# Constant products on TensorE around the router of a two-layer decoder trunk: 25 for 14 ahead of the rank products, and nine new ones behind them

## The chip, the cores and the metric

The kernel runs on one core of one Trainium2 chip. The metric is the device time of one execution in microseconds (us), lower is better. TensorE (PE in the profile) multiplies, VectorE (DVE) and ScalarE (ACT) work on vectors, GpSimd (POOL) is nearly unused, and SyncE (SP) issues the loads of the weights.

## The reference, cut to what matters

All of it is float32, with 256 tokens, a width of 1024, two layers, and 32 experts in 4 groups of 8.

```python
for l in range(DEPTH):                       # DEPTH = 2
    x = x + token_mixers(rms_norm(x, norm_mix_g[l]), ...)
    h = rms_norm(x, norm_ffn_g[l])
    glog = h @ rg_w + rg_b                   # 4 group logits, the best group is taken
    elog = h @ re_w + re_b                   # 32 expert logits, the best 2 of that group are taken
    # every token goes to its two experts; the tokens of an expert are ordered (rank within the expert)
    # expert e, for its tokens:  (silu(xb @ w_gate[e]) * (xb @ w_up[e])) @ w_down[e]
    # the weighted results are added to x
return rms_norm(x, norm_final_g)
```

## The kernel before, in words

Every engine has a program of its own that runs in the order in which it is written; semaphores join them. A layer has two parts. The first, the mixers, multiplies by the combined projection and its successors (function `product`, line 1362). The second is the mixture of experts: all 32 experts are gone through in pairs of experts, 16 pairs a layer, each with 64 places for tokens, and one more passage of the same loop where an expert has more tokens. The weights of a pair are 12 blocks of 1 MB, loaded by SP (line 502) into a ring of 18 slots. SP loads into a slot again when TensorE has counted `pair_freed` for it (lines 461 and following).

The change lies between the two parts, in `tensor_program` (from line 1338). In the order in which TensorE has it, for each layer:

- `norm_transposes(1)` (line 1392) transposes `x`.
- 16 products of the router (line 1578) give the 36 logits of each token in psC, and count `route_ps`. VectorE waits for that and works out the groups and the experts of each token in a chain of small operations, lines 1162 to 1194. The last of them writes `member`, a table of tokens by experts, and counts `members`. In the trace `member` has the name `ycT_parts`, and the tables beside it have the name `ycT`.
- `spin(14)` (function at line 1374, body at line 1377) makes 14 products of the constants `ones` and `before` (128x128 each) into the first quarter of psD's second half, `psD[:, 1, 0:128]`. Nobody reads it; the next to write there is the pair's own turning of its selection (line 1654), on TensorE too.
- TensorE waits for `members`, and makes five rank products (line 1586) into the first half of psD, and counts `rank_ps`.
- VectorE, which has meanwhile worked out the weights of the experts (lines 1197 to 1203), waits for `rank_ps`, writes the place of each token (line 1226) and the selection of the first pair, `sel` (line 1209; `sel_mem` in the trace), and counts `sel_ready`.
- TensorE waits for `sel_ready` and gathers the tokens of the first pair: 16 products (`gather(0)` and `gather(1)`, line 1603) from `xn` and `sel_mem`. ScalarE wrote `xn` before (line 721).
- It goes on with the pairs (function `pair`): the gate and up products (line 1614), the turned selection (line 1654), and so on. `pair_freed` is counted for the first time behind the first 16 products of line 1614.

A float32 product stands in the trace as two passes of TensorE, each with its weight load (PEld) and its matmul (PE). So 14 constants have 28 rows, and the 16 products of the first gather have 32.

Of the kernel before, what the change touches and what calls it, by code (L numbers as in the profile page):

```python
# [50 lines left out]
def build_trunk(nc, x_in, positions, norm_mix_g, norm_ffn_g, norm_final_g, w_in, gmlp_ws, gmlp_b, conv_w,  # L51
# [114 lines left out]
    with ExitStack() as ctx:  # L166
# [1172 lines left out]
        def tensor_program(pe):  # L1339
# [6 lines left out]
            for l in range(DEPTH):  # L1346
# [27 lines left out]
                def spin(n):  # L1374

                    for _ in range(n):
                        te.matmul(psD[:, 1, 0:P], ones[:, :], before[:, :], start=True, stop=True)
# [200 lines left out]
                        ins = te.matmul(psC[:, t, 0:N_ROUTE], hT[:, c, t * P:(t + 1) * P], r_w[:, c, :],  # L1578
                                        start=c == 0, stop=c == KC - 1)
                ins.then_inc(route_ps, 1)  # L1580
                spin(14)

                pe.wait_ge(members, l + 1)
                for o, w, t, start, stop in ((0, before_r, 0, True, True), (1, ones_r, 0, True, False), (1, before_r, 1, False, True),
                                             (2, ones_r, 0, True, False), (2, ones_r, 1, False, True)):
                    ins = te.matmul(psD[:, 0, o * NE:(o + 1) * NE], w[:, :], member[:, t, :], start=start, stop=stop)
                ins.then_inc(rank_ps, 1)

                def expert_arrived(i, p, tail):

                    s = OVER_SLOTS[p] if tail else pair_slot(i, p)
                    count = l * LOADS[s] + (LOADS[s] + i if tail else (i * PAIR_SLOTS + p) // SLOTS + 1)
                    if s in OVER_SLOTS:
                        count = count + over
                    pe.wait_ge(landed[s], count * 16)
                    return s
# [115 lines left out]
        @block.tensor  # L1712
        def _(pe):
            tensor_program(pe)
# [23 lines left out]
```

## Time and profile before

| | |
|---|---|
| median of 3 runs | 1457.68 us (1456.96 to 1458.08) |
| time of the profiled execution | 1455.0 us |
| its span, first to last instruction | 1453.2 us |
| TensorE, matmuls busy | 1390.3 us, 96% |
| VectorE busy | 559.2 us, 38% |
| ScalarE busy | 357.8 us, 25% |
| loaded and stored | 490.18 MB, mean 337 GB/s |
| mean granted clock of TensorE | 0.988 of full speed |

The busy share of TensorE says little of what bounds the kernel, since it is nearly full in every stage. What counts is what each stage waits for last. The granted clock is 1.00 for TensorE at its full clock of 2.4 GHz and 0.50 at half of it, 1.2 GHz; numbers between the two are means over a stretch in which it changed.

### The profile page before, as it was taken

Reading aid. Unit: us, or ns where it says so; the run is one execution under the profiler, and the core shown is the slowest. Engines: PE = TensorE matmul, PEld = TensorE weight load, DVE = VectorE, ACT = ScalarE, POOL = GpSimd, SP = SyncE. Lnnn points to the kernel's source line nnn. Section 1 sums busy time; section 2 is a strip of 40 time slices with the busy share of each in tenths; the row PEclk is TensorE's granted clock in tenths of the full one; section 3 lists DMA queues with packets and bytes.
Section 4 is the critical chain, followed back from the end, with each engine's and each line's share of the span. In section 5 each row is a group of like instructions: output and inputs, shape, how many; then the busy total and the mean of one; then the engine's idle time right before and its main releaser. Section 6 shows DMA issues by size and latency. Waiting matters only on the chain.

```text
span 1453.2 us, 17629 instructions
## 1 busy us (share of the span) xinstructions
PE 1390.3 (96%) x7295; PEld 836.8 (58%) x7295; DVE 559.2 (38%) x882; ACT 357.8 (25%) x532; POOL 6.3 (0%) x36
## 2 busy tenths in 40 slices
PE   6999999899999999999889999998999999999996
PEld 5899887644444444443378988885444444444442
DVE  6686645522222222221277857454222222222123
ACT  5554432211111111111155444431111111111111
POOL 0000000000000000000000000000000000000000
PEclk9999999999999999999989999999999999999999
DMA  8655757699999999999946457586999999999995
GB/s 278 208 184 174 264 199 291 255 389 421 421 421 421 421 421 421 421 421 422 407 152 217 164 189 274 185 347 261 414 421 421 421 421 421 421 421 421 421 421 221
DMA packets 101123, 490.18 MB, mean 337 GB/s; under 512 B 8716, under 2 KB 12084, under 8 KB 51892
## 3 DMA queue, kind: packets, MB, share of 16 engines
q1 hardware_dynamic: 99940, 488.72, 84.3%
q8 instruction: 58, 0.95, 0.3%
q10 hardware_dynamic: 1104, 0.34, 0.1%
q14 instruction: 21, 0.17, 0.0%
HBM read 487.98 MB, written 1.05 MB: 337 GB/s over the span
## 4 chain that ended last, share of the span: by engine, by line
PE 66%; SPq 18%; DVE 8%; DMA 4%; issue 2%; ACT 1%; DVEq 0%; ACTq 0%
PE psB L1614 19%; SPq L502 18%; PE psA L1362 12%; PE psB L1362 12%; PE psC L1625 10%; PE psA L1603 6%; DMA slot<-in_expert_w_down_dram 4%; DVE parts L926 2%; PE psA L1639 2%; PE psA L1640 1%; DVE score_work L1021 1%; DVE top L1020 1%; PE psD L1666 1%; ACT parts L731 1%; PE psC L1578 0%
## 5 line engine op out<-in xcount | busy, mean ns | idle before, releaser
L1614 PE MATMUL psB<-slot,uT 128*64 128x512 f32 x2048 | 459.4, 595 | 3.4 <-DMA slot<-in_expert_w_up_dram 3.4
L1614 PEld LDWEIGHTS psB<-slot,uT 128*64 128x64 f32 x2048 | 142.4, 137 | 271.7 <-issue 268.7
L1625 PE MATMUL psC<-slot,ybT_plain 128*64 128x512 f32 x1024 | 228.1, 596 | 4.8 <-ACT ybT_plain L839 2.7
L926 DVE TENSOR_TENSOR parts<-slot,parts 128x2048 fp32r<-128x2048 f32 (+1 forms) x80 | 177.4, 2249 | 70.1 <-ACT parts L731 69.8
L731 ACT ACTIVATE parts<-slot 128x2048 fp32r<-128x2048 f32 (+1 forms) x80 | 147.9, 1880 | 92.7 <-PE psA L1362 50.1
L1625 PEld LDWEIGHTS psC<-slot,ybT_plain 128*64 128x64 f32 x1024 | 71.2, 137 | 137.8 <-issue 131.2
L1242 DVE TENSOR_TENSOR x<-x,psA 128x1024 f32<-128x1024 f32 x62 | 75.7, 1221 | 189.5 <-PE psA L1640 189.5
L1603 PEld LDWEIGHTS psA<-sel_mem,xn 128*128 128x128 f32 x1024 | 124.6, 199 | 27.0 <-issue 25.7
L1362 PE MATMUL psB<-parts,hT_parts 128*128 128x512 f32 x448 | 138.9, 391 | 0.2
L1603 PE MATMUL psA<-sel_mem,xn 128*128 128x128 f32 x1024 | 133.0, 286 | 2.5 <-DVE sel_mem L1209 2.5
L1258 DVE TENSOR_TENSOR low_y_parts<-psC,low_y_parts 128x512 fp32r<-128x512 f32 x64 | 41.2, 686 | 235.4 <-ACT low_y_parts L842 235.4
L1362 PE MATMUL psA<-parts,hT_parts 128*128 128x512 f32 (+1 forms) x384 | 113.5, 378 | 2.3 <-DVE low_y_parts L959 2.3
L842 ACT ACTIVATE low_y_parts<-psC 128x512 fp32r<-128x512 f32 x64 | 34.8, 595 | 264.9 <-PE psC L1625 264.9
L1362 PEld LDWEIGHTS psB<-parts,hT_parts 128*128 128x128 f32 x448 | 83.4, 188 | 18.5 <-DVE tmp L1133 1.0
L1253 DVE SCALAR_TENSOR_TENSOR ybT_plain<-score_work,slot_w,psB 128x512 f32<-128x512 f32 x32 | 23.9, 747 | 171.0 <-PE psB L1614 170.7
L1362 PE MATMUL psB<-parts,low_y_parts 128*128 128x512 f32 x224 | 87.2, 389 | 0.0
L833 ACT ACTIVATE w_sum<-psD 64x4 f32<-64x4 f32 x64 | 10.7, 168 | 289.7 <-PE psD L1654 289.3
L1362 PEld LDWEIGHTS psA<-parts,hT_parts 128*128 128x128 f32 x384 | 70.3, 188 | 14.9 <-issue 2.8
L1235 DVE TENSOR_TENSOR uT<-psA,g_ffn 128x512 f32<-128x512 f32 x64 | 44.3, 692 | 90.0 <-PE psA L1603 90.0
L1362 PE MATMUL psA<-parts,low_y_parts 128*128 128x512 f32 (+1 forms) x192 | 72.3, 376 | 0.0
L839 ACT ACTIVATE ybT_plain<-psD 128x512 f32<-128x512 f32 x32 | 19.1, 597 | 175.0 <-PE psD L1666 175.0
L1639 PE MATMUL psA<-low_y_parts,selT 128*128 128x512 f32 x124 | 55.4, 447 | 4.0 <-DVE low_y_parts L1258 4.0
(300 smaller groups left out, 1185.5 us busy)
## 6 DMA issues: line engine op xcount, KB each, us to landing
slot<-in_expert_w_gate_dram SPq DMA_DIRECT2D x128, 1024.0 KB, 21.4
slot<-in_expert_w_up_dram SPq DMA_DIRECT2D x128, 1024.0 KB, 20.6
slot<-in_expert_w_down_dram SPq DMA_DIRECT2D x128, 1024.0 KB, 22.5
slot<-in_w_in_dram SPq DMA_DIRECT2D x56, 1024.0 KB, 5.1
slot<-in_w_out_dram SPq DMA_DIRECT2D x8, 1024.0 KB, 5.0
slot<-in_w_proj_b_dram SPq DMA_DIRECT2D x4, 1024.0 KB, 4.9
slot<-in_w_proj_c_dram SPq DMA_DIRECT2D x4, 1024.0 KB, 5.0
slot<-in_w_proj_a_dram SPq DMA_DIRECT2D x4, 1024.0 KB, 4.9
```

The source lines that it names most:

```text
L502: sp.dma_start(dst, src).then_inc(done_sem, 16)
L731: sc.activation(high_and_low(i)[0], mix_slot(i), ACT.Copy).then_inc(high_act, 1)
L842: sc.activation(y_high[:, n, :], psC[:, n, :], ACT.Copy).then_inc(y_act, 1)
L926: v.tensor_tensor(low_part, mix_slot(i), high_part, ALU.subtract).then_inc(low_dve, 1)
L1235: v.tensor_tensor(xT[:, 4 * b:4 * b + 4, :], psA[:, b, :].rearrange("p (c n) -> p c n", c=4), g_ffn[:, 4 * b:4 * b + 4].unsqueeze(2).to_br ...
L1242: v.tensor_tensor(x[:, t, :].rearrange("p (b n) -> p b n", b=2), x[:, t, :].rearrange("p (b n) -> p b n", b=2), (psB if last and t else ps ...
L1258: v.tensor_tensor(y_low[:, n, :], psC[:, n, :], y_high[:, n, :], ALU.subtract).then_inc(y_dve, 1)
L1362: ins = te.matmul(o, first, second, start=start and i == 0, stop=stop and i == len(TERMS) - 1)
L1603: ins = te.matmul(psA[:, b, (c % 4) * P:(c % 4 + 1) * P], xn[:, o:o + P], sel_plain[:, t, :], start=t == 0, stop=t == NT - 1)
L1614: ins = te.matmul(psB[j * BLK:(j + 1) * BLK, o, :], xT[:, 4 * half + c, j * BLK:(j + 1) * BLK], w[:, c, :], start=half == 0 and c == 0, st ...
L1625: ins = te.matmul(psC[j * BLK:(j + 1) * BLK, n, :], hidT[:, 2 * k + c, j * BLK:(j + 1) * BLK], w[:, c, n * 512:(n + 1) * 512], start=k == ...
L1639: te.matmul(ps[:, n, :], selT[:, t, :], y_high[:, n, :], start=True, stop=False)
```

## The change

It makes 25 products of constants ahead of the wait for `members` in place of 14, and adds nine behind the rank products, ahead of the first gather.

```diff
                 ins.then_inc(route_ps, 1)
-                spin(14)
+                spin(25)
 
                 pe.wait_ge(members, l + 1)
                 for o, w, t, start, stop in ((0, before_r, 0, True, True), (1, ones_r, 0, True, False), (1, before_r, 1, False, True),
                                              (2, ones_r, 0, True, False), (2, ones_r, 1, False, True)):
                     ins = te.matmul(psD[:, 0, o * NE:(o + 1) * NE], w[:, :], member[:, t, :], start=start, stop=stop)
                 ins.then_inc(rank_ps, 1)
+                spin(9)
```

On TensorE the order of the products between the router and the first pair was this, in each layer (`ycT_parts` is `member`):

```order
L1578 MATMUL psC<-r_w,hT 128x36 x16
L1377 MATMUL psD<-before,ones 128x128 x14
L1586 MATMUL psD<-ycT_parts,before_r 128x32
L1586 MATMUL psD<-ycT_parts,ones_r 128x32
L1586 MATMUL psD<-ycT_parts,before_r 128x32
L1586 MATMUL psD<-ycT_parts,ones_r 128x32 x2
L1603 MATMUL psA<-sel_mem,xn 128x128 x16
```

In the changed program, where the lines behind the addition have numbers higher by one, it is this:

```order
L1578 MATMUL psC<-r_w,hT 128x36 x16
L1377 MATMUL psD<-before,ones 128x128 x25
L1586 MATMUL psD<-ycT_parts,before_r 128x32
L1586 MATMUL psD<-ycT_parts,ones_r 128x32
L1586 MATMUL psD<-ycT_parts,before_r 128x32
L1586 MATMUL psD<-ycT_parts,ones_r 128x32 x2
L1377 MATMUL psD<-before,ones 128x128 x9
L1604 MATMUL psA<-sel_mem,xn 128x128 x16
```

Eleven constants more stand ahead of the rank products, and nine between them and the gather. Nothing else moved on any engine.

## Rows read from the trace of the kernel before

**Rows 1.** The page: span, and the chain that ended last, by engine.
```profile
span 1453.2 us, 17629 instructions
...
PE 66%; SPq 18%; DVE 8%; DMA 4%; issue 2%; ACT 1%; DVEq 0%; ACTq 0%
```

**Rows 2.** Windows: stretch, width, busy of PE, PEld, DVE, ACT, POOL; clock, DMA share, GB/s.
```profile
270.00:280.00 10.00, 10.00 (x50) 5.07 (x49) 1.34 (x2) 0.00 (x0) 0.00 (x0) 0.89 0.25 66
...
300.00:310.00 10.00, 10.00 (x46) 3.41 (x44) 2.51 (x3) 1.09 (x2) 0.00 (x0) 1.00 0.94 368
650.00:660.00 10.00, 10.00 (x64) 5.90 (x62) 2.13 (x3) 0.60 (x1) 0.00 (x0) 1.00 1.01 419
...
680.00:690.00 10.00, 8.11 (x39) 2.88 (x37) 0.75 (x1) 0.60 (x1) 0.00 (x0) 1.00 1.01 421
```

**Rows 3.** Timeline, first layer: start, duration, engine, line, tiles [idle before, releaser].
```profile
255.78 3.76 PE L1578 MATMUL psC<-r_w,hT 128*128 128x36 f32 x32
257.37 4.20 ACT L721 ACTIVATE xn<-x,rstd 128x1024 f32<-128x1024 f32 x2 [0.82 <-DVE rstd L908]
...
259.38 3.37 PE L1377 MATMUL psD<-before,ones 128*128 128x128 f32 x28
259.65 0.41 DVE L1162 SCALAR_TENSOR_TENSOR ycT<-psC,rstd,r_b 128x32 f32<-128x32 f32 x2 [2.31 <-PE psC L1578]
...
264.16 0.28 PE L1586 MATMUL psD<-ycT_parts,before_r 128*128 128x32 f32 x1 [1.41 <-DVE ycT_parts L1194]
...
264.51 0.37 PE L1586 MATMUL psD<-ycT_parts,ones_r 128*128 128x32 f32 x2
...
265.34 0.22 DVE L1226 SCALAR_TENSOR_TENSOR ycT<-psD,ycT_parts 128x64 f32<-128x64 f32 x1
265.59 0.43 DVE L1209 TENSOR_TENSOR sel_mem<-ycT,slots 128x256 fp32r<-128x256 f32 x1
...
266.16 6.70 PE L1603 MATMUL psA<-sel_mem,xn 128*128 128x128 f32 x32 [1.27 <-DVE sel_mem L1209]
...
272.79 7.09 PE L1614 MATMUL psB<-slot,uT 128*64 128x512 f32 x32
```

**Rows 4.** Timeline, the same place in the second layer.
```profile
978.74 5.00 PE L1377 MATMUL psD<-before,ones 128*128 128x128 f32 x28
...
983.78 0.28 PE L1586 MATMUL psD<-ycT_parts,before_r 128*128 128x32 f32 x1
...
985.69 3.84 PE L1603 MATMUL psA<-sel_mem,xn 128*128 128x128 f32 x32 [1.18 <-DVE sel_mem L1209]
```

**Rows 5.** Windows of 1 us in which the granted clock fell or rose.
```profile
263.00:264.00 1.00, 0.00 (x0) 0.00 (x0) 0.90 (x8) 0.21 (x1) 0.00 (x0) 1.00 0.94 393
265.00:266.00 1.00, 0.00 (x0) 0.00 (x0) 0.93 (x6) 0.00 (x0) 0.00 (x0) 0.70 0.08 33
266.00:267.00 1.00, 0.84 (x4) 0.87 (x5) 0.52 (x4) 0.00 (x0) 0.00 (x0) 0.50 0.00 0
...
272.00:273.00 1.00, 1.00 (x9) 0.86 (x9) 0.11 (x1) 0.00 (x0) 0.00 (x0) 0.89 0.00 0
292.00:293.00 1.00, 1.00 (x9) 1.00 (x9) 0.30 (x1) 0.46 (x1) 0.00 (x0) 0.85 0.99 418
296.00:297.00 1.00, 1.00 (x6) 0.28 (x4) 0.36 (x1) 0.00 (x0) 0.00 (x0) 0.94 1.06 442
978.00:979.00 1.00, 1.00 (x10) 1.00 (x10) 0.00 (x0) 1.00 (x2) 0.00 (x0) 0.89 1.01 418
...
982.00:983.00 1.00, 1.00 (x10) 1.00 (x9) 0.70 (x6) 0.26 (x1) 0.00 (x0) 0.90 1.00 418
```

**Rows 6.** The chain that ended last, in order of time, first pair of the first layer.
```profile
272.86 7.02 PE psB L1614 x32
279.88 0.39 PE psD L1654 x2
280.28 0.43 DVE sel_mem L1209
...
290.95 0.76 DVE ybT_plain L1253
291.75 0.75 PE psD L1666 x4
```

## The prediction

> **What bounds the kernel now.** I began with the page. The chain that ended last is two thirds TensorE and a fifth SP's queue [rows 1], so neither the loads nor TensorE bound it alone, and I asked in which stage each of them ends last. For that I went to the windows of 10 us over the first layer's experts. From 650 to 660 us, as in all the windows before it from 310 us on, the DMA engines are full at about 420 GB/s; at 680 to 690 us they still are, and TensorE has only 8.11 of 10 us of work [rows 2]. So the end of the layer is set by the loads. But at 270 to 280 us the DMA engines moved only 66 GB/s, and at 300 to 310 us they have a second small gap [rows 2]. The ring is full there and SP waits for TensorE to free slots. Since the amount that remains to be loaded is fixed, every microsecond by which TensorE reaches the first pair later comes out at the end of the layer, and every one by which it is earlier is won. Work between the first pair and that second gap does not swallow it: VectorE's long chain of tables starts only when line 1654 of the first pair is done (280.28), and it is this chain that TensorE waits for at 291.75 [rows 6]. The whole piece moves with the first gather.
>
> Then I read the timeline of the passage that the change touches, to see who ends last at each step. In the first layer TensorE ends its 28 constant passes at 259.38 + 3.37 = 262.75, stands idle for 1.41 us, makes the rank products from 264.16 to 264.88, and stands idle for 1.27 us until the selection is there; the gather starts at 266.16 [rows 3]. Both waits are for VectorE. In the second layer the constants take 5.00 us instead of 3.37 and end at 983.74, right at the rank products; the gather starts at 985.69 [rows 4].
>
> Last I read the granted clock. In the first layer it is full while TensorE idles at 263 to 264, falls during the second idle stretch (0.70 over 265 to 266), and stays at 0.50, which is 1.2 GHz, until 272 [rows 5]. The gather takes 6.70 us there against 3.84 at the full clock in the second layer [rows 3, 4]. That is 2.86 us that idling costs. In the second layer the fall comes at another place, at the end of the router's products, with TensorE busy around it (0.89 over 978 to 979), and the clock is back in the window of 982 [rows 5]. It cost nothing, since it only slowed constants that had time.
>
> **The change, part by part.** It adds 11 constants ahead of the rank products and 9 behind them, in each layer. Nothing is removed and no load is issued otherwise.
>
> Price of one constant: 3.37 us for 28 passes is 0.120 us a pass, 0.241 us a constant [rows 3]. At half clock 28 passes of the second layer took 5.00 us, most of them slow [rows 4]; so 1.63 us is what one such fall adds.
>
> The 11: 22 passes x 0.120 = 2.65 us. They have 1.41 us of idle time to lie in [rows 3], and run over it by 1.24. In the first layer they end at 262.75 + 2.65 = 265.40. Queued behind them on TensorE stand the rank products, and for these VectorE waits. They take 0.72 us (264.16 to 264.88) and so end at 266.12. VectorE started 0.11 us behind TensorE's end at line 1162 (259.54 to 259.65); with as much here, line 1226 starts at 266.23 in place of 265.34, later by 0.89, because 0.46 us of VectorE's own work on the expert weights used to lie there as cover. Line 1209 then ends at 266.02 + 0.89 = 266.91, and TensorE could gather 0.14 us later, at 267.05 [rows 3].
>
> The 9: 18 passes x 0.120 = 2.17 us from 266.12, so until 268.29. What waits behind them is the gather itself. It starts at 268.29 and not at 266.16: **+2.13 us** at full clock. ScalarE's `xn`, which the gather also needs, is done at 261.57 [rows 3].
>
> What they may give back: with TensorE busy without a break from the router to the gather, I expect no fall in front of the gather. It then takes 3.84 us, and ends at 272.13, where it ended at 272.86 [rows 3, 4]: **-0.73 us** in the first layer.
>
> The second layer: the constants end at 983.74 + 2.65 = 986.39, the rank products at 987.11, the nine at 989.28. The gather starts there in place of 985.69: **+3.59 us**, and was at full clock already, so nothing comes back [rows 4].
>
> TensorE: Matmul & The Clock Gate, the page of the Trainium skill, section "Back-to-back issue gap", gives about 81 ns a matmul with its weight load at 128 columns, sustained. The trace has 120 ns for a float32 pass, so the trace disagrees with it, and its own number is used. By the page's figure 50 passes would take an estimated 4.05 us, all before `members`, the nine would end some 0.2 us behind the selection, and the sum would be -2.5 us.
>
> Sum against the profiled execution's own 1455.0 us, with the falls where they were: -0.73 + 3.59 = **+2.86 us**. The median of the runs stands 2.68 us above that execution, so where the clock fell in them is not known to me. With no fall in either layer before or after, the sum is 2 x 2.13 = +4.26 us. The place of the falls differs between the two layers for the same instructions, so it isn't tied to them. I take the middle of the two sums, **+3.5 us**, and the median of 1457.68 gives 1461.2 us. The ends: both layers like the second one, 2 x 3.59 = +7.2 us; both like the first one, 2 x -0.73 = -1.5 us.
>
> **The rivals.** A measurement of this kernel can tell about 0.2%, 2.9 us, from no change.
>
> *Both gathers were slow in the timed runs.* For it: one more slow gather in them (2.86 us) would explain that their median is 2.68 us above the profiled execution. Against it: two falls at other places would too. It gives -1.5 us, 1456.2 us.
>
> *Faster: half clock that outlasts the gather.* The place is the first gather and the gate and up products behind it. From 266.16 until the clock is back at 272.2 there are some 6.0 us at half clock, and they cost 2.86, that is 0.47 a microsecond. The constants cost 4.26 us over both layers; to win 2.9 beside that, each layer must get back 3.6 us, so from about 7.6 us of half clock behind the start of the gather on, this case decides. With 10 us in both layers it gives 4.26 - 9.4 = -5.1 us, 1452.5 us. For it: the timed runs are slower than the profiled one. Against it: the traced stretches are about 6.6 us (265.6 to 272.2) and 3.4 us (978.8 to 982.2, and 292.7 to 296.1) [rows 5], and none is longer.
>
> *The delay is swallowed.* The second gap of the DMA engines could absorb it, or loads end the first pairs later than I read. Against it stand the two gaps [rows 2] and the chain [rows 6]. It gives 0 to +1 us, 1458.2 us.
>
> *Constants that pack closer than those before.* If the 22 added passes fit in the 1.41 us of idle time and the nine behind the ranks in theirs, both waits hide them; that needs 0.064 us a pass where the row has 0.120 [rows 3]. Then only the saved gather remains, -2.86 us, 1454.8 us. No row supports it. The figure of the Trainium skill's page TensorE: Matmul & The Clock Gate quoted above points to this case.
>
> **How the numbers follow.** The forecast's family, +2.86 to +7.2 us with its middle near +3.5: 0.68, of which 0.57 lies above 2.9 us and 0.11 just below. Both gathers slow before: 0.14. Faster by the long half clock: 0.09. Delay swallowed: 0.08. Closer packing: 0.01. So slower by over 0.2% has 0.57; within 0.2% has 0.11 + 0.14 + 0.08 + 0.01 = 0.34; faster by over 0.2% has 0.09. The range runs from the case of two slow gathers, 1456.2, to both layers like the second one, 1464.9; the fast rival is left out.
>
> **What would show each step.** In the profile after, line 1377 should have 136 passes in place of 56, about 0.120 us each. The first rank product should stand directly behind the constants without an idle stretch, some 6.0 us behind the router's products (7.6 if the clock fell there). The gather should stand directly behind the nine, 2.17 us behind the rank products, and should take 3.84 us in both layers with the clock at 1.00. VectorE's line 1226 should wait for TensorE about 0.9 us longer than before. The DMA gap ahead of the first pair should be longer by 2.1 us wherever the gather was fast before. I am wrong if the gathers are still slow with TensorE busy ahead of them (then the change only costs, +5 us), if the traces before had slow gathers in both layers (then the time is equal or lower), or if the end of the layer doesn't move with the first gather.

## The result: 3 us slower

| | before | changed |
|---|---|---|
| median, 20 runs each | 1456.44 us (1452.7 to 1458.39) | 1459.7 us (1454.47 to 1465.3) |
| ratio | 1 | 1.0022, 95% interval 1.0012 to 1.0033 |
| profiled execution | 1455.0 us, span 1453.2 | 1462.01 us, span 1460.3 |

The changed kernel is slower by 3.2 us (0.22%, interval 1.7 to 4.8 us); the forecast was +3.5. Its runs also spread over 10.8 us where those of before spread over 5.7, so one profiled execution each, 7 us apart, overstates the difference.

The page of the changed kernel: its span, and the shares of the chain that ended last, by line. PE psD L1377, the constants, stands in it; in the chain of the kernel before it is not among the lines listed.

```profile
span 1460.3 us, 17789 instructions
...
SPq L502 20%; PE psB L1615 17%; PE psA L1362 13%; PE psB L1362 12%; PE psC L1626 9%; PE psA L1604 5%; DMA slot<-in_expert_w_down_dram 4%; DVE parts L926 2%; PE psA L1640 2%; PE psD L1377 1%; PE psA L1641 1%; DVE score_work L1021 1%; DVE top L1020 1%; PE psD L1667 1%; ACT parts L731 1%
```

The constants, which nothing waited for in the first layer before, are now part of what sets the end. The timeline of the same passage in the first layer, changed kernel, as [rows 3]:

```profile
257.97 3.96 PE L1578 MATMUL psC<-r_w,hT 128*128 128x36 f32 x32
...
261.74 7.28 PE L1377 MATMUL psD<-before,ones 128*128 128x128 f32 x50
...
268.77 0.26 PE L1586 MATMUL psD<-ycT_parts,before_r 128*128 128x32 f32 x1
...
269.33 2.25 PE L1377 MATMUL psD<-before,ones 128*128 128x128 f32 x18
269.52 0.23 DVE L1226 SCALAR_TENSOR_TENSOR ycT<-psD,ycT_parts 128x64 f32<-128x64 f32 x1 [1.71 <-PE psD L1586]
...
271.42 3.74 PE L1604 MATMUL psA<-sel_mem,xn 128*128 128x128 f32 x32
...
275.09 7.09 PE L1615 MATMUL psB<-slot,uT 128*64 128x512 f32 x32
```

And in the second layer, as [rows 4]:

```profile
982.71 8.55 PE L1377 MATMUL psD<-before,ones 128*128 128x128 f32 x50
...
991.76 0.23 DVE L1226 SCALAR_TENSOR_TENSOR ycT<-psD,ycT_parts 128x64 f32<-128x64 f32 x1 [2.72 <-PE psD L1586]
...
993.66 3.74 PE L1604 MATMUL psA<-sel_mem,xn 128*128 128x128 f32 x32
```

Three things are to be seen. VectorE now waits for the rank products, 1.71 and 2.72 us, where it started without an idle stretch before [rows 3]. The rank products and the gather stand directly behind the constants, without idle time. And the 50 passes take 7.28 and 8.55 us, not the 6.0 of full clock. The windows of 1 us say why (columns as in [rows 5]):

```profile
261.00:262.00 1.00, 1.00 (x8) 1.00 (x8) 0.00 (x0) 1.00 (x2) 0.00 (x0) 0.69 0.99 410
262.00:263.00 1.00, 1.00 (x6) 1.00 (x7) 0.81 (x6) 1.00 (x1) 0.00 (x0) 0.50 1.00 418
264.00:265.00 1.00, 1.00 (x8) 1.00 (x7) 0.80 (x5) 1.00 (x1) 0.00 (x0) 0.60 1.08 442
...
271.00:272.00 1.00, 1.00 (x12) 1.00 (x11) 0.00 (x0) 0.00 (x0) 0.00 (x0) 1.00 0.00 0
...
981.00:982.00 1.00, 1.00 (x10) 1.00 (x8) 0.00 (x0) 1.00 (x1) 0.00 (x0) 0.80 1.05 434
...
988.00:989.00 1.00, 1.00 (x9) 1.00 (x9) 0.88 (x5) 0.00 (x0) 0.00 (x0) 0.79 0.02 8
```

The clock falls to 1.2 GHz with TensorE fully busy, near the end of the router's products: from 261.4 to 264.8 us, 3.4 us, in the first layer, and from 981.6 to 988.4, 6.8 us, in the second. Both gathers run at full clock. The loads pay for the delay. At 270 to 280 us, in the first row below, they move 10 GB/s where they moved 66, and at 300 to 310 us 286 where they moved 368 [rows 2]. Counted in half microseconds with under 210 GB/s, the gap ahead of the first pair is 11.5 to 12.0 us where the gather of the kernel before was fast (three layers out of two traces; the second traces are told of below), and 14.0 to 15.5 us in the four of the changed kernel; the prediction had 2.1 us more.

```profile
270.00:280.00 10.00, 10.00 (x71) 6.74 (x71) 2.09 (x6) 0.00 (x0) 0.00 (x0) 1.00 0.05 10
300.00:310.00 10.00, 10.00 (x48) 3.44 (x46) 1.47 (x3) 1.09 (x2) 0.00 (x0) 1.00 0.76 286
```

### The profile page after: what moved, and what is told of

Its sections match the earlier page's. It is cut to its first block, busy times and chain, and to the rows that moved or that the text cites. A ratio compares the mean times of both kernels' runs of the same rounds, so it can differ in the third digit from the quotient of the medians.

```text
span 1460.3 us, 17789 instructions
## 1 busy us (share of the span) xinstructions
PE 1401.3 (96%) x7375; PEld 847.9 (58%) x7375; DVE 559.5 (38%) x882; ACT 358.0 (25%) x532; POOL 6.3 (0%) x36
## 4 chain that ended last, share of the span: by engine, by line
PE 64%; SPq 21%; DVE 8%; DMA 4%; issue 2%; ACT 1%; DVEq 0%; ACTq 0%
SPq L502 20%; PE psB L1615 17%; PE psA L1362 13%; PE psB L1362 12%; PE psC L1626 9%; PE psA L1604 5%; DMA slot<-in_expert_w_down_dram 4%; DVE parts L926 2%; PE psA L1640 2%; PE psD L1377 1%; PE psA L1641 1%; DVE score_work L1021 1%; DVE top L1020 1%; PE psD L1667 1%; ACT parts L731 1%
## 5 line engine op out<-in xcount | busy, mean ns | idle before, releaser
L1604 PEld LDWEIGHTS psA<-sel_mem,xn 128*128 128x128 f32 x1024 | 120.0, 193 | 24.3 <-issue 24.3
L1604 PE MATMUL psA<-sel_mem,xn 128*128 128x128 f32 x1024 | 128.1, 279 | 0.0
L1362 PE MATMUL psA<-parts,hT_parts 128*128 128x512 f32 (+1 forms) x384 | 116.5, 386 | 1.9 <-DVE low_y_parts L959 1.9
```

Source lines behind the costliest of these rows:

```text
L1362: ins = te.matmul(o, first, second, start=start and i == 0, stop=stop and i == len(TERMS) - 1)
L1604: ins = te.matmul(psA[:, b, (c % 4) * P:(c % 4 + 1) * P], xn[:, o:o + P], sel_plain[:, t, :], start=t == 0, stop=t == NT - 1)
```

## The experiments

Two measures serve for all of them. One is the ratio of the timed runs to the kernel before on the same chip. The other is the **stretch** in each layer's trace from the start of the router's first product to the end of the first gather. For before it is 272.86 - 255.78 = 17.08 us in the first layer and 989.53 - 975.15 = 14.38 in the second; for the changed kernel 17.19 and 18.82. A **passage** is this part of one layer in one trace, so every trace has two.

| constants (ahead, behind) | median, us | ratio, interval | stretch, layers 1 and 2 | gathers, us |
|---|---|---|---|---|
| 14, 0 (before) | 1456.44 | 1 | 17.08, 14.38 | 6.70, 3.84 |
| 14, 0 again | one run | | 14.43, 14.81 | 3.81, 3.84 |
| 25, 9 (changed) | 1459.7 | 1.0022 (1.0012 to 1.0033) | 17.19, 18.82 | 3.74, 3.74 |
| 25, 9 again | one run | | 17.20, 17.19 | 3.74, 3.74 |
| 25, 0 | 1457.77 | 1.0010 (0.9996 to 1.0024) | 16.19, 17.76 | 3.81, 3.84 |
| 14, 9 | 1457.13 | 1.0005 (0.9992 to 1.0017) | 15.12, 15.08 | 3.74, 3.74 |
| none | 1459.9 | 1.0022 (1.0008 to 1.0036) | 15.91, 17.64 | 5.25, 6.46 |
| 36, 18 | 1468.36 | 1.0082 (1.0067 to 1.0098) | 23.29, 21.66 | 3.74, 3.74 |
| 25, 9, and 5 ahead of the transposes | 1460.52 | 1.0027 (1.0015 to 1.0040) | 18.82, 17.19 | 3.74, 3.74 |
| 14, 5 | 1454.41 | 0.9985 (0.9975 to 0.9994) | 14.60, 15.77 | 3.81, 4.63 |
| 14, 5, and 5 ahead of the transposes | 1454.62 | 0.9987 (0.9977 to 0.9996) | 15.47, 14.62 | 3.74, 3.84 |
| 14, 5, and 7 among the router's | 1456.2 | 0.9996 (0.9985 to 1.0007) | 15.76, 15.94 | 3.81, 3.84 |
| 14, 5, and 3 among the router's | 1457.35 | 1.0000 (0.9992 to 1.0009) | 16.18, 16.45 | 4.55, 4.70 |

### One part of the change alone

```diff
-                spin(14)
+                spin(25)
```

> 25 constants ahead of the rank products, none behind. Theory (the queue delay counts one for one): at full clock the gather starts 7.7 us behind the start of the constants in place of 6.8, so +0.9 us a layer and about +1.8 us in all; each fall of the clock in the constants adds up to 1.6 us a layer. Rival (the nine do all the harm): no difference from before beyond 0.3 us. Rival (delay swallowed): the gather starts later, but the time is the same.

It measured +1.5 us (interval -0.6 to +3.5). The gather starts 12.38 and 13.92 us into the stretch; with the nine it starts at 13.45 and 15.08. The 25 cost 50 passes of 7.5 and 8.6 us, and at most 4.9 us of that is covered: so long TensorE stands idle there in the kernel without constants (below).

```diff
                 ins.then_inc(rank_ps, 1)
+                spin(9)
```

> 14 constants ahead, nine behind the rank products. Theory: the rank products start as before, the nine end 2.2 us behind them, so the gather starts 7.7 us behind the start of the constants in place of 6.8: +0.9 us a layer, +1.8 us in all, less 2.9 us for each slow gather that is avoided; so between -1 and +2 us. A gather is then at full clock (3.8 us) in both layers unless the clock fell in the idle time ahead of the rank products. Rival (the 25 do all the harm): as before in time.

It measured +0.7 us (interval -1.2 to +2.5). The 28 passes end, slowed, at 8.59 us of the stretch and the rank products start at 8.71 and 8.67, so nothing is late there. The nine move the gather to 11.38 and 11.34, where the kernel before has it at 10.38 to 10.97. Against the mean of those four, 10.63, the 25 alone move the gather by 1.75 and 3.29 us and the nine alone by 0.75 and 0.71. So both parts delay the gather, the 25 more than the nine; "the 25 do all the harm" and "the nine do all the harm" are both out by the traces. The timed runs can't share the time out between them: +1.5 and +0.7 us come to 2.2 of the 3.2, and either interval includes no change.

### No constants

```diff
-                spin(14)
```

> No constants at all: TensorE idles 4.6 us ahead of the rank products and 1.3 us ahead of the gather. Theory: nothing is queued ahead of the gather, but it runs at half clock in both layers, 6.7 us each, and some of the gate and up products too; 3 to 6 us over before less what before itself loses to slow gathers: +1.5 to +4 us. Rival (the clock of this passage is worth nothing, the constants never paid): same time as before or lower.

It measured +3.2 us (interval 1.2 to 5.2): the 14 constants do pay. The two stretches come to 33.55 us against 30.35 for an execution of the kernel before (mean of two traces), also +3.2. Timeline and windows of this kernel, first layer (line 1602 is the gather):

```profile
266.75 0.40 PE L1585 MATMUL psD<-ycT_parts,before_r 128*128 128x32 f32 x1 [4.62 <-DVE ycT_parts L1194]
...
268.87 5.25 PE L1602 MATMUL psA<-sel_mem,xn 128*128 128x128 f32 x32 [0.87 <-DVE sel_mem L1209]
```

```profile
261.00:262.00 1.00, 1.00 (x9) 0.99 (x8) 0.00 (x0) 1.00 (x2) 0.00 (x0) 0.83 1.03 426
265.00:266.00 1.00, 0.00 (x0) 0.00 (x0) 0.82 (x8) 0.28 (x2) 0.00 (x0) 0.50 0.96 401
270.00:271.00 1.00, 1.00 (x7) 1.00 (x6) 0.00 (x0) 0.00 (x0) 0.00 (x0) 0.50 0.05 16
271.00:272.00 1.00, 1.00 (x7) 1.00 (x7) 0.00 (x0) 0.00 (x0) 0.00 (x0) 0.55 0.00 0
```

The clock falls at the router here as well, and with TensorE idle for 4.62 us it does not come back. It stays at half for 10.2 us here, from 261.7 to 271.9, which is 3.0 us into the gather, and for 13.7 us in the second layer. The gathers take 5.25 and 6.46 us, less than the 6.7 expected. With 14 constants in that place the clock was back after 3.4 us in seven of the eight passages with this fall, and after 6.8 in one. So what the constants do, by this comparison, is bring a fallen clock back.

### The change doubled

```diff
-                spin(14)
+                spin(36)
...
                 ins.then_inc(rank_ps, 1)
+                spin(18)
```

> 36 constants ahead and 18 behind the rank products, 20 more constants a layer than the changed kernel. Theory: 40 passes more of 0.120 us, 4.8 us a layer, all in front of the gather, so +9.6 us over the changed kernel's 1459.7, about 1469. The gathers take 3.8 us each. Rival (delay swallowed by the loads later): under half of it, below 1464.

It measured +11.9 us on before (1.0082), 8.7 us more than the changed kernel. 40 passes a layer more, of 0.120 us, are 9.6 us over both layers. So what is queued ahead of the gather comes out at the end nearly one for one, and little of it is swallowed later.

### The kernel before, a second trace

> The kernel before once more, for a second trace of its two passages. In eleven of the twelve passages traced so far the clock fell 2.6 to 4.0 us behind the router's first product; the one that it spared had the slow gather. Theory: the fall at the router comes in both layers, the 28 passes then take about 5.0 us and end at the rank products, and the gathers take 3.8 us; the stretch from the router's first product to the gather's end is 14.4 us. Rival (slow gathers are usual in the kernel before): 17.1 us in both layers, with the gather at 6.7 us.

One run, 1455.95 us. Its timeline, second layer, and two windows there:

```profile
974.81 4.20 PE L1578 MATMUL psC<-r_w,hT 128*128 128x36 f32 x32
978.82 4.58 PE L1377 MATMUL psD<-before,ones 128*128 128x128 f32 x28
983.87 0.28 PE L1586 MATMUL psD<-ycT_parts,before_r 128*128 128x32 f32 x1 [0.47 <-DVE ycT_parts L1194]
...
985.78 3.84 PE L1603 MATMUL psA<-sel_mem,xn 128*128 128x128 f32 x32 [1.18 <-DVE sel_mem L1209]
```

```profile
977.00:978.00 1.00, 1.00 (x12) 1.00 (x11) 0.00 (x0) 1.00 (x1) 0.00 (x0) 0.98 1.02 426
979.00:980.00 1.00, 1.00 (x6) 1.00 (x6) 0.73 (x5) 1.00 (x1) 0.00 (x0) 0.50 1.05 426
```

The fall at the router is in both layers, and both gathers are fast. So of the four passages of the kernel before, three have the fall at the router, where it moves the start of the gather little (10.54, 10.62 and 10.97 us into the stretch, against 10.38 in the passage without it), and one has the slow gather that I had built the gain on.

### Is idle time ahead of the transposes to blame?

```diff
+                spin(5)
                 norm_transposes(1)
...
-                spin(14)
+                spin(25)
...
                 ins.then_inc(rank_ps, 1)
+                spin(9)
```

> The changed kernel with five more constants ahead of the transposes of x, in the 1.3 us for which TensorE waits there. Theory (the fall at the router follows that idle time): the fall goes or gets rare, 50 passes take 6.0 us, the gather starts 8.9 us behind the start of the constants in both layers, and the time is 1 to 3 us below the changed kernel's, about 1457.5. Rival (the transposes and the narrow products of the router bring the fall by themselves): the 50 passes still take 7.3 to 8.6 us, and the time is the changed kernel's, about 1459.7.

My theory fell, and the rival's numbers held. The timeline of the first layer:

```profile
254.27 1.27 PE L1377 MATMUL psD<-before,ones 128*128 128x128 f32 x10
255.75 1.16 PE L1392 MATMUL psA<-ident,x 128*128 128x128 f32 x8 [0.20 <-DVE x L1154]
...
257.66 4.40 PE L1579 MATMUL psC<-r_w,hT 128*128 128x36 f32 x32
261.86 8.47 PE L1377 MATMUL psD<-before,ones 128*128 128x128 f32 x50
```

The idle time of 1.31 us is down to 0.20, and the clock still fell, here for 6.8 us. The time is that of the changed kernel (1.0027 and 1.0022).

### Five constants behind the rank products

```diff
                 ins.then_inc(rank_ps, 1)
+                spin(5)
```

> 14 constants ahead and five behind the rank products. Theory: 10 passes take 1.2 us of the 1.2 to 1.3 us that TensorE idles ahead of the gather, so nothing is later, and no gather is slow: the time is that of before less the slow gathers, -0.5 to -2 us. Rival (slow gathers are too rare in before to matter): the same time as before.

It measured 1454.41 us, -2.2 us on before (interval -3.6 to -0.9), so it beats both kernels, by a little. The first layer is a passage with the fall at the router: the 28 passes end in time, the ten behind end 0.07 us ahead of the gather, and the stretch is 14.60. The second is a passage without that fall, and there the clock fell at 982.7 us, 1.0 us behind the end of 1.67 us of idle time. TensorE's timeline and two windows show it:

```profile
981.73 0.28 PE L1586 MATMUL psD<-ycT_parts,before_r 128*128 128x32 f32 x1 [1.67 <-DVE ycT_parts L1194]
...
982.31 2.13 PE L1377 MATMUL psD<-before,ones 128*128 128x128 f32 x10
984.24 4.63 PE L1604 MATMUL psA<-sel_mem,xn 128*128 128x128 f32 x32
```

```profile
982.00:983.00 1.00, 1.00 (x10) 1.00 (x10) 0.90 (x6) 0.00 (x0) 0.00 (x0) 0.85 0.04 16
983.00:984.00 1.00, 1.00 (x6) 1.00 (x6) 0.90 (x5) 0.00 (x0) 0.00 (x0) 0.50 0.00 0
```

The five don't prevent that fall but they use up part of it: the gather takes 4.63 us and not 6.70.

Where the 2.2 us are won stays open. The two stretches come to 30.37 us, and those of the kernel before to 30.35 an execution, so the traces show no gain up to the gather. The mean granted clock of the timed runs is higher, 0.9889 (12 runs) against 0.9874 (28 runs of the kernel before beside them). By 2 x 0.0015 x 1455 that is an estimated 4 us less at half clock in an execution, and it doesn't tell where.

> As 14 and five, with five more constants ahead of the transposes of x. Theory: if the early five prevent the fall at the router, the 28 passes take 3.4 us and leave 1.4 us of idle time ahead of the rank products, in which the clock can fall for the gather; no better than 14 and five alone. If they don't prevent it, the same as 14 and five. In both cases within 1 us of before. Rival (any constant in idle time helps): 2 us or more below before.

Its edit is the one above and this:

```diff
+                spin(5)
                 norm_transposes(1)
```

It measured -1.9 us (interval -3.3 to -0.6), the same as without them, though not within the 1 us of before that I had worked out; the 28 passes took 6.18 us in its first layer, so the fall came there too.

### A second trace of the changed kernel

> The changed kernel once more, for a second trace of its two passages. Theory: the clock falls at the router in both layers, and the stretch from the router's first product to the gather's end has one of three lengths: 15.8 us without a fall, 17.2 us with a fall of 3.4 us, 18.8 us with one of 6.8 us. Rival (the long stretch of the second layer in the first trace was something else than the clock): lengths between these.

The two stretches are 17.20 and 17.19, the 50 passes 7.5 us in both, at 1458.26 us. With the first trace that makes four passages of four with the fall at the router, three with the short stretch and one with the long. No trace has the 15.8 of no fall.

### What brings the fall at the router?

```diff
                     for t in range(NT):
                         ins = te.matmul(psC[:, t, 0:N_ROUTE], ...)
+                    if c < KC - 1:
+                        spin(1)
...
                 ins.then_inc(rank_ps, 1)
+                spin(5)
```

> 14 and five, and one constant behind each of the router's first seven pairs of products: 14 passes more, 1.7 us a layer on the path. Theory (the narrow products of the router, 36 columns each, leave the clock without enough work): the fall 2.6 to 4.0 us behind the router's first product is gone in both layers. Rival (the fall is due to the idle time and the transposes ahead of the router): it comes as before, 2.6 to 4.0 us behind the first product.

The fall is gone in both layers. TensorE's timeline and windows of the first:

```profile
257.83 0.53 PE L1578 MATMUL psC<-r_w,hT 128*128 128x36 f32 x4
258.20 0.47 PE L1377 MATMUL psD<-before,ones 128*128 128x128 f32 x2
...
262.22 3.37 PE L1377 MATMUL psD<-before,ones 128*128 128x128 f32 x28
```

```profile
260.00:261.00 1.00, 1.00 (x12) 1.00 (x11) 0.00 (x0) 1.00 (x2) 0.00 (x0) 1.00 1.01 418
263.00:264.00 1.00, 1.00 (x12) 1.00 (x11) 0.70 (x8) 1.00 (x1) 0.00 (x0) 1.00 1.00 410
266.00:267.00 1.00, 0.00 (x1) 0.00 (x1) 0.90 (x7) 0.21 (x1) 0.00 (x0) 1.00 0.12 41
```

The 28 passes take 3.37 us again, and the gather 3.81. The kernel was then timed:

> The kernel with one constant behind each of seven pairs of router products, and 14 and five, timed. Theory: with the clock up from the router to the gather the stretch to the gather's end is 15.8 us in both layers, 1.7 of it for the constants in the router, where 14 and five alone have 14.4 to 15.8 us; so about +1 to +2 us on 14 and five if nothing else changes, about 1456, the time of before. Rival (a clock kept up here also spares falls later, at 290 and at 1010 us, as its one trace shows): 2 to 4 us below before.

> The same with constants behind three of the router's eight pairs of products only, 0.7 us a layer. Theory (enough work per time keeps the clock up, with a threshold between none and seven): if the fall at the router is gone, the stretch is 14.8 to 15 us and the time 1 us below the kernel with seven; if it still comes, the 28 passes at the lower clock end 0.2 us behind the members and the time is that of 14 and five plus 1.4 us.

With seven among the router's products: -0.6 us (interval -2.2 to +1.0), and some 1.6 us above 14 and five, as worked out. The single run ahead of it, 1453.21 us, was no measure. The rival, 2 to 4 us below before, stands at the very end of the interval. The mean granted clock of these 12 runs was the highest of all, 0.9920, and yet the time is not clearly below before, which fits the 1.7 us a layer that its constants add to the path. With three (`if c in (1, 3, 5)` in the same place, so behind the second, fourth and sixth pair): no difference from before (interval -1.2 to +1.3). TensorE's timeline of its first layer:

```profile
261.65 3.37 PE L1377 MATMUL psD<-before,ones 128*128 128x128 f32 x28
266.43 0.28 PE L1588 MATMUL psD<-ycT_parts,before_r 128*128 128x32 f32 x1 [1.41 <-DVE ycT_parts L1194]
...
269.02 4.55 PE L1606 MATMUL psA<-sel_mem,xn 128*128 128x128 f32 x32
```

Three were enough to keep the clock up at the router in both layers; the fall then came behind the idle time ahead of the rank products, 267.3 to 270.7, and slowed the gather. I had not foreseen that case: the time is some 1.2 us above the kernel with seven where I had it 1 us below. Why the kernel with seven, whose idle times are the same, was spared it in four passages of four stays open.

## Why the prediction held, point by point

**What bounds.** Right. The end moves with the first gather: the doubled change shows it (8.7 us for 9.6 queued), and the emptier windows of the loads fit it.

**The price of a constant.** Right: 3.37 us for 28 passes in every trace at full clock. The Trainium skill, TensorE: Matmul & The Clock Gate, "Back-to-back issue gap", has about 81 ns for a matmul with its load at 128 columns; the traces disagree, at 120 ns for a float32 pass. The same page's section "LDWEIGHTS (loading the stationary operand)" has columns / 1.2 ns for the load, 107 ns for 128. That is nearer, and it fits that the router's passes, with 36 columns moving, take as long as the constants' with 128 (3.76 us for 32, which is 0.118 us each).

**Queued behind the 25 and the nine.** Right in kind and, at full clock, in size. The nine move the gather by 1.07 and 1.16 us (13.45 against 12.38, 15.08 against 13.92), worked out as 268.29 - 267.05 = 1.24. By themselves they stand in the timeline with 2.25 us, the last pass beside the gather's first; worked out 2.17.

**"With TensorE busy without a break from the router to the gather, I expect no fall in front of the gather."** Half right. The gathers take 3.74 us in four passages of four. But the clock fell anyway, at the router and with TensorE busy, in all four. Being busy there did not prevent a fall.

**The term that was mis-sized** is the 2.65 us for the 22 added passes, at full clock. The fall makes the 50 passes 7.3 to 8.6 us long where I had 6.0. The -0.73 us of the first layer measured +0.11 (17.19 against 17.08), and the +3.59 of the second +4.44 (18.82 against 14.38) in one trace. In the second trace both layers have a fall of 3.4 us and stretches of 17.2, 2.4 to 2.8 us above those of the second trace of before. I had counted a fall in the added passes as a sign only (7.6 us for the 50), and put no term for it into the sum. For the same reason VectorE's wait for the rank products grew to 1.71 and 2.72 us and not to 0.9.

**The slow gather as a gain.** Over-weighted. I gave it back in one layer of two; it stood in one passage of four of the kernel before. The link is what I missed. The fall at the router makes the 28 passes 4.6 to 5.0 us long (6.2 once), and these leave at most 0.47 us of the idle time ahead of the rank products. In all of the 18 traced passages that have constants behind the router and the fall at the router, the gather is at full clock (3.74 to 3.84 us). The two without that fall, the first layer of before and the second of 14 and five, had the slow gather. That the one spares the other is argued and not shown: of the six passages in which constants among the router's products kept the clock up, with the same idle time behind, two had a slow gather and four had none.

**The sum.** The four stretches of the changed kernel sum to 70.4 us, those of before to 60.7. That is +4.85 us for one execution of two layers, more than the timed +3.2. Part of it comes back later, and I take that as an estimate only. In the gather of the second pair, where TensorE idled just before [rows 6], the clock fell in all four passages of before and in one of four of the changed kernel; 16 passes took 3.33 and not 2.05 us in before's second layer:

```profile
1003.86 2.05 PE L1603 MATMUL psA<-sel_mem,xn 128*128 128x128 f32 x16
...
1009.18 3.33 PE L1603 MATMUL psA<-sel_mem,xn 128*128 128x128 f32 x16
```

That is 0.75 x 2 x 1.3 = 1.9 us back, and leaves +2.9. The traces that show it are few, and no run tested it. The timed runs agree with it in one number: their mean granted clock is 0.9892 in the changed kernel (20 runs) and 0.9873 to 0.9874 in the kernel before (three sets of 23 to 29 runs), so an execution of the changed kernel spends an estimated 5 us less at half clock (2 x 0.0018 x 1455), although its falls at the router are no shorter.

So it is partly luck that +3.5 met +3.2. Up to the gather the change cost 4.85 us in the traces where my two sums had 2.86 and 4.26, since the fall lengthens the constants and a slow gather to be saved is rarer than I took it; and some 1.9 us that I had not looked for came back behind it.

Two readings in the prediction are a little off. The half clock of the first layer begins at 265.4 us and lasts 6.8 us (0.70 over 265 to 266), not 265.6 and 6.6. And VectorE's cover is 0.35 us, which is what its own 1.24 - 0.89 gives; 0.46 is the whole gap from the end of the rank products to line 1226.

**The rivals.** Slow gathers in both layers of the timed runs: unlikely, since three of the four traced were fast, but no timed run beyond these two was traced. Half clock that outlasts the gather: not in before; in this passage stretches of that length (10.2 and 13.7 us) were seen only without constants. Delay swallowed: out, by the doubled change. Closer packing: out, at 0.120 us a pass in every trace at full clock.

## What to carry to other kernels

Work that nobody reads is free only while it ends before what is queued behind it becomes ready. 25 constants take 6.0 us at full clock and 7.3 to 8.6 with a fall, where at most 4.9 us were idle; nine take 2.2 us where 1.2 to 1.3 were. Together they cost 3.2 us, while 14 ahead and five behind, which fit, were 2.2 us faster than 14 alone. Reckon with the lower clock too when sizing such work: the same 28 passes took 3.4 us without a fall and 4.6 to 6.2 with one. No count between 14 and 25 or below 14 was run, other than none. Where the clock varies from run to run, take a second trace of the kernel before; one trace made a passage in four look like one in two.

## What the runs showed of the hardware

The clock fell with TensorE fully busy in matmul rows. The router's products have 36 columns moving, and each pass takes 0.118 us where one with 128 takes 0.120. In 18 of 20 passages whose router had nothing in between and constants behind it, and in both without constants, the clock fell 2.9 to 4.0 us behind the router's first product. Filling the idle time ahead of the transposes did not change that (a fall in all four passages of those two kernels). A constant behind seven or even three of the eight pairs of products ended it, in six passages of six. What in them does it was not separated: they also lengthen the router by 0.7 and 1.7 us, none with few columns was put there, and the 16 transposes stand ahead of the router in every kernel. A row with TensorE at 1.00 busy is no sign of a clock at 1.00 (1.00 busy at a clock of 0.50 over 979 to 980 us in the second trace of before).
